# Expert weights of a MoE block: loads that take fourteen places in rotation, with two places more

## The reference

```
g_sel     = argmax(h @ w_router_group + b)             # one of 4 groups per token
top_idx   = top_k(e_logits of that group, 2)           # two of its 8 experts per token
for e in 32 experts:
    ys[e] = (silu(x_e @ w_gate[e]) * (x_e @ w_up[e])) @ w_down[e]   # 1024 -> 256 -> 1024
out       = x + sum over the two experts of weight * ys
result    = rmsnorm(out)
```

## Time and profile before

| | us |
|---|---|
| median of 3 runs (lowest, highest) | 1531.02 (1529.89, 1532.00) |
| profiled execution | 1532.88 |
| its span, first to last instruction | 1531.1 |
| PE busy in the span | 1417.8 (93%) |
| DVE busy | 898.7 (59%) |
| ACT busy | 620.6 (41%) |
| DMA, mean over the span | 248 GB/s |

### The profile page before, as it was taken

How to read it: one execution, slowest core, us unless ns; L and a number is a source line. 1 busy time by engine, 2 the same in 40 slices (tenths; PEclk the granted TensorE clock), 3 DMA queues, 4 the chain that set the end, 5 groups by cost and what they waited for, 6 DMA issues and landing times.

```text
span 1531.1 us, 26859 instructions
## 1 busy us (share of the span) xinstructions
PE 1417.8 (93%) x11511; PEld 1272.0 (83%) x11511; DVE 898.7 (59%) x1043; ACT 620.6 (41%) x739; POOL 19.2 (1%) x24
## 2 busy tenths in 40 slices
PE   4999999999999999999999999999999999985665
PEld 2899998988999989999999899999997989652323
DVE  2777776547877777777775555556567644320002
ACT  2444345545444354344443443444444643320002
POOL 0000000400000000000000000000000000000000
PEclk9899999999999999999999999999999999998879
DMA  8898884515988849788654355554534349799996
GB/s 308 276 324 301 303 306 165 198 56 200 324 306 301 296 165 329 274 287 307 202 167 164 111 195 190 192 176 136 175 108 147 129 157 405 308 422 421 421 421 267
DMA packets 203911, 380.33 MB, mean 248 GB/s; under 512 B 12725, under 2 KB 158010, under 8 KB 192058
## 3 DMA queue, kind: packets, MB, share of 16 engines
q1 hardware_dynamic: 203834, 379.22, 69.1%
HBM read 378.14 MB, written 1.05 MB: 248 GB/s over the span
## 4 chain that ended last, share of the span: by engine, by line
PE 80%; DMA 9%; DVE 5%; ACT 3%; issue 2%; SPq 1%; ACTq 0%; DVEq 0%
PE ps L678 18%; PE ps L680 17%; PE ps L679 17%; PE ps L706 10%; DMA plain_whi<-in_w_exp_down_dram 7%; PE ps L707 5%; PE ps L1427 2%; ACT whi L1540 2%; DVE wlo L1964 2%; DMA ada_raw<-in_w_ada_dram 1%; PE ps L1400 1%; PE ps L1383 1%; SPq L561 1%; PE ps L846 1%; PE ps L793 1%
## 5 line engine op out<-in xcount | busy, mean ns | idle before, releaser
L1964 DVE TENSOR_TENSOR wlo<-raw,whi 128x2048 fp32r<-128x2048 f32 (+1 forms) x188 | 425.5, 2263 | 241.2 <-ACT whi L1540 241.1
L1540 ACT ACTIVATE whi<-raw 128x2048 fp32r<-128x2048 f32 (+1 forms) x188 | 354.7, 1887 | 175.4 <-PE ps L680 146.7
L678 PE MATMUL ps<-h_both,whi 128*128 128x256 f32 x1320 | 380.4, 288 | 1.2 <-DVE wlo L1964 0.9
L680 PE MATMUL ps<-h_both,wlo 128*128 128x256 f32 x1320 | 374.5, 284 | 0.0
L679 PE MATMUL ps<-h_both,whi 128*128 128x256 f32 x1320 | 374.4, 284 | 0.0
L678 PEld LDWEIGHTS ps<-h_both,whi 128*128 128x128 f32 x1320 | 252.0, 191 | 9.4 <-issue 4.5
L706 PE MATMUL ps<-h_both,whi 128*128 128x512 f32 x704 | 254.8, 404 | 2.1 <-DVE h_both L1974 2.1
L679 PEld LDWEIGHTS ps<-h_both,whi 128*128 128x128 f32 x1320 | 252.2, 191 | 0.7 <-issue 0.5
L680 PEld LDWEIGHTS ps<-h_both,wlo 128*128 128x128 f32 x1320 | 252.1, 191 | 0.0
L678 PE MATMUL ps<-hidhi,whi 128*128 128x256 f32 x704 | 201.2, 286 | 2.1 <-DVE wlo L2101 2.1
L680 PE MATMUL ps<-hidhi,wlo 128*128 128x256 f32 x704 | 199.3, 283 | 0.0
(11 more groups left out here) (325 smaller groups left out, 1851.4 us busy)
## 6 DMA issues: line engine op xcount, KB each, us to landing
ada_raw<-in_w_ada_dram SPq DMA_DIRECT2D x72, 1024.0 KB, 5.4
raw<-in_ffn_wg_dram SPq DMA_DIRECT2D x44, 1024.0 KB, 6.0
raw<-in_ffn_wu_dram SPq DMA_DIRECT2D x44, 1024.0 KB, 5.4
raw<-in_ffn_wd_dram SPq DMA_DIRECT2D x44, 1024.0 KB, 6.3
raw<-in_w_in_dram SPq DMA_DIRECT2D x18, 1024.0 KB, 5.3
raw<-in_w_exp_down_dram SPq DMA_DIRECT2D x14, 1024.0 KB, 19.0
plain_whi<-in_w_exp_gate_dram SPq DMA_DIRECT2D x14, 1024.0 KB, 19.0
plain_wlo<-in_w_exp_gate_dram SPq DMA_DIRECT2D x14, 1024.0 KB, 16.9
```

Of the source, the lines that this page charges most:

```text
L678: pe.matmul(o, wh, xh, start=start, stop=False, skip_group_check=shared)
L680: return pe.matmul(o, wl, xh, start=False, stop=stop, skip_group_check=shared)
L1540: act.activation(whi[s][:, 0:width], raw[s][:, 0:width], ACT.Copy).then_inc(high[s], 1)
L1964: dve.tensor_tensor(wlo[s][:, 0:width], raw[s][:, 0:width], whi[s][:, 0:width].bitcast(F32), ALU.subtract).then_inc(split[s], 1)
```

## The change

The program now reserves 2 KB of each partition of SBUF for DMA descriptors (`dynamic_dma_scratch_size=2048` in the call at L2634, where no size was given before), and two places of 8 KB each, `spare[0]` and `spare[1]`, are allocated. Three things follow in the order of the loads.

First, the loads of GATE(0) for j = 0 and 1 go into the two spare places, and SP issues them between units of `blk2`, behind u = 20 and u = 22. Before, they stood behind u = 30.

Second, in round 1 the loads of UP for j = 1 and 2 go into `ar(0)` and `ar(4096)`, which held those of GATE(0) before. They wait for no product, only for the landing of the load of round 0 that has the same semaphore.

Third, from UP(1), j = 3 on, the loads take fourteen places (`ring`) in turn. Load m of this rotation waits for the product that last read its place (`ring_user`), and for the landing of the load before on its own semaphore. In the old code a load waited for the product of its own kind in the round before.

```diff
+        spare = [sb(f"spare{i}", [P, UW]) for i in range(2)]
...
-        first_w = [[ar(0, UW), ar(4096, UW), ar(6144, UW), plain_over("exps")],
+        first_w = [[spare[0][:, :], spare[1][:, :], ar(6144, UW), plain_over("exps")],
...
-                    [h_area[1], ar(6144, UW), raw[2][:, :], ada_raw[:, 0, :]],
-                    [ada_raw[:, 1, :], raw[0][:, :], raw[1][:, :], split_area["whi2"]]]
-        later_w = [[split_area[name] for name in ("wlo2", "whi0", "wlo0", "whi1")],
-                   [split_area["wlo1"], ar(6144, UW), raw[2][:, :], ada_raw[:, 0, :]],
-                   [ada_raw[:, 1, :], raw[0][:, :], raw[1][:, :], split_area["whi2"]]]
+                    [h_area[1], ar(0, UW), ar(4096, UW)]]
+        ring = [spare[0][:, :], spare[1][:, :], ar(6144, UW), raw[2][:, :], ada_raw[:, 0, :], ada_raw[:, 1, :]] + \
+               [split_area[name] for name in ("whi0", "wlo0", "whi1", "wlo1")] + \
+               [raw[0][:, :], raw[1][:, :], split_area["whi2"], split_area["wlo2"]]
+        RING_AT = 12 + 4 * UP + 3
...
+        def ring_user(m):
+
+            if m < len(ring):
+                return (((GATE, 1),) * 3 + ((UP, 1),) * 3 + ((GATE, 2),) * 4 + ((DOWN, 1),) * 4)[m]
+            q, rest = divmod(m - len(ring) + RING_AT, 12)
+            return rest // 4, q + 1
...
+            for u in range(31):
+                load_unit("blk2", u)
+                if u in (20, 22):
+                    expert_load(0, GATE, u // 2 - 10)
+
             sp.wait_ge(sem("o_split"), 8)
-            expert_load(0, GATE, 0)
-            expert_load(0, GATE, 1)
+            expert_load(0, GATE, 2)
             load_unit("blk2", 31)
-            expert_load(0, GATE, 2)
             expert_load(0, GATE, 3)
...
-            expert_load(1, UP, 0)
-            sp.wait_ge(expert_used[GATE], 1)
-            expert_load(1, UP, 1)
-            sp.wait_ge(expert_used[UP], 1)
-            expert_load(1, UP, 2)
-            expert_load(1, UP, 3)
-            expert_load(1, DOWN, 0)
-            sp.wait_ge(expert_used[DOWN], 1)
-            for j in range(1, 4):
-                expert_load(1, DOWN, j)
-            for q in range(2, NQ):
-                for kind in (GATE, UP, DOWN):
-                    sp.wait_ge(expert_used[kind], q)
-                    for row in ((0, 1) if kind == DOWN and q == NQ - 1 else (None,)):
-                        for j in range(4):
-                            expert_load(q, kind, j, row=row)
+            for j in range(3):
+                sp.wait_ge(expert_landed[UP][j], 16)
+                expert_load(1, UP, j)
+            for m in range(ring_index(NQ, GATE, 0)):
+                q, rest = divmod(m + RING_AT, 12)
+                kind, j = divmod(rest, 4)
+                user, uses = ring_user(m)
+                sp.wait_ge(expert_used[user], uses)
+                sp.wait_ge(expert_landed[kind][j], 16 * q)
+                expert_load(q, kind, j, row=0 if (q, kind) == (NQ - 1, DOWN) else None)
+            for j in range(4):
+                expert_load(NQ - 1, DOWN, j, row=1)
```

More of the change, by code:

```diff
@@ L287, in build, with ring_index @@
         second_w = [[split_area[name] for name in ("whi0", "wlo0", "whi1", "wlo1")],
-                    [h_area[1], ar(6144, UW), raw[2][:, :], ada_raw[:, 0, :]],
-                    [ada_raw[:, 1, :], raw[0][:, :], raw[1][:, :], split_area["whi2"]]]
-        later_w = [[split_area[name] for name in ("wlo2", "whi0", "wlo0", "whi1")],
-                   [split_area["wlo1"], ar(6144, UW), raw[2][:, :], ada_raw[:, 0, :]],
-                   [ada_raw[:, 1, :], raw[0][:, :], raw[1][:, :], split_area["whi2"]]]
-        def expert_w(q, kind, j):
-            return (first_w, second_w, later_w)[min(q, 2)][kind][j]
+                    [h_area[1], ar(0, UW), ar(4096, UW)]]
[3 more added lines that the diff above has]
+        RING_AT = 12 + 4 * UP + 3
+        def ring_index(q, kind, j):
+            return 12 * q + 4 * kind + j - RING_AT
+        def expert_w(q, kind, j):
+            if q == NQ:
+                q = NQ - 1
+            m = ring_index(q, kind, j)
+            if m >= 0:
+                return ring[m % len(ring)]
+            return (first_w, second_w)[q][kind][j]
+        def ring_user(m):
[3 more added lines that the diff above has]
+            return rest // 4, q + 1
         y_hi = sb_over("y_hi", "hf", 0, [P, D])
@@ L547, in _ @@
             dense("ffn3", 1, 1, None)
-            for u in range(31):
-                load_unit("blk2", u)
             def expert_load(q, kind, j, e=None, row=None):
@@ L2632 @@
     from concourse.bass_utils import run_bass_kernel_spmd as _run
-    nc = _bacc.Bacc("TRN2", target_bir_lowering=False, num_devices=1)
+    nc = _bacc.Bacc("TRN2", target_bir_lowering=False, num_devices=1, dynamic_dma_scratch_size=2048)
     arrays, aps = {}, {}
```

## The result

| | before | after |
|---|---|---|
| median of 5 runs each (lowest, highest), us | 1531.02 (1529.89, 1533.31) | 1523.75 (1520.24, 1525.04) |
| profiled execution, us | 1532.88 | 1525.04 |
| its span, us | 1531.1 | 1523.2 |

The ratio is 0.9948, with a 95% interval of 0.9935 to 0.9961. The median is 7.3 us lower; 1524.4 had been forecast, and 1523.75 was measured. Busy times are the same within 0.6 us (PE 1417.2, DVE 898.7, ACT 620.1 us), so nothing is computed faster.

What follows compares the result with a forecast made beforehand. The end of a byte stream at 421 GB/s was taken to bound the kernel. Two loads (5.0 us) plus closed holes (1.6 us) make 6.6 us less, 1524.4 us against the median of 1531.02; 8-in-10 range 1521.5 to 1527.5.

Steps and rivals of the forecast that it cites:

- What bounds the kernel: At the kernel's end, a stream of bytes at 421 GB/s bounds; the 13.6 us after the last landing stay untouched.
- The unit: In the load stream, one load of 1024 KB takes the full stream 2.49 us at 421 GB/s.
- Part 1: Two GATE(0) loads issued early in blk2: cost nothing and give nothing; the stream would stand idle longer before 1314.
- Part 2: Before GATE(0): two more UP(1) loads issued, 5.0 us less stream behind 1314; dead stretch begins at 1311 or 1312.
- Part 3: At the restart after GATE(0): more loads released, two holes close, 1.05 us and 0.58 us, 1.6 us together.
- Part 4: In the rotation up to GATE(2)'s end near 1361: the queue just lasts, 0.3 us to spare, nothing lost.
- the first rival: Around 1363: PE brings GATE(2) late and the stream goes dry; 1526 to 1527.5 us; chance 0.09.
- Part 5: The 2 KB descriptor area in SBUF: loads run on a hardware queue, so its effect is taken as 0.
- The sum: Whole kernel: 5.0 + 1.6 = 6.6 us less, 1524.4 against the median; bounds 5.0 and about 9.
- Slow issuing: In the rotation: a deeper queue makes SP's issues set the pace; 1536.7 us at 2.65 per load; chance 0.04.
- The loads of UP(1) got out: Before 1314: the rival said an earlier wait holds these two loads, only holes gained; 1529.4 us; chance 0.04.
- signs of being wrong: Wrong if the GATE(0) product itself moved, the rate fell below 421, or the stream went dry in a later round.

Runs made afterwards that it cites:

- e5: The changed kernel, but the load of UP(1), j = 2 waits for GATE(0); 1525.21 us in one run.
- e6: The changed kernel, but the loads of UP(1), j = 1 and 2 wait for GATE(0); 1528.15 us in one run.
- e1: The changed kernel, but the first two loads of GATE(0) are issued at their old place behind unit 30 of blk2; 1523.30 us, ratio to before 0.9956.
- e2: The kernel before, with only the spare places, the 2 KB area and the early issue of two GATE(0) loads; 1531.67 us, ratio 1.0005.
- e7: The changed kernel, but the second and third of the three loads that GATE(0) releases wait for UP(0); 1526.14 us in one run.
- e11: The kernel of e7 once more, unchanged; 1526.96 us in one run.
- e9: The changed kernel once more, with a profile; 1523.42 us in one run.
- e3: The changed kernel, but from round 2 on each load also waits for its own kind's product in the round before; 1526.46 us, ratio to before 0.9972.
- e8: The kernel before once more, with a profile; 1529.49 us in one run.
- e4: The changed kernel, but five eighths of the load of UP(1), j = 3 go ahead of the wait for GATE(0); 1524.86 us, ratio to before 0.9959.

## Why the prediction was right

*What bounds the kernel.* Right: the last landing fell by what the stream gained, and what follows it took 13.5 us as before.

*The unit, 2.49 us.* Right: 2.58 and 5.07 us at the end of the bytes for one and two loads (e5, e6). On the 358 GB/s that the prediction sets beside it, the same page of the Trainium skill ("DMA: Bandwidth & Descriptors", section on measured bandwidth) is fuller than the prediction tells: it gives 358 GB/s for a core when both cores of the pair stream. For a single core whose neighbour is idle it gives 425 GB/s, measured for a transfer of 16 MB, and the 421 of this program, which uses one core, agree with that.

*Part 1, the early issue at nothing.* Right in the time, from both sides (e1, e2). The idle time came in the front and not, as I had it, as a longer dead stretch (e2). This was the step at which the plain reading of the change, two loads earlier, two loads gained, would have come out right by chance and for a wrong reason.

*Part 2, 5.0 us.* Right: 5.07 (e6). The dead stretch began at about 1311, as forecast.

*Part 3, 1.6 us.* Nearly right: with both loads of UP(1) held back, the end of the bytes is still 203.83 - 202.52 = 1.3 us ahead of before. The hole of the restart alone is 0.9 to 1.1 (e7, e11), where 1.05 was forecast. The second hole, put at 0.58, has no run of its own.

*Part 4, nothing lost at 1361.* Right, and in the profile of after with more room than I had worked out. GATE(2) ended at 1354.45 + 3.63 = 1358.1 and not at 1361, 1.2 us of it from the start of GATE(0), and the rest because PE's clock was less low on the way. The same window of before and then of after (PE busy, granted clock, DMA share, GB/s):

```profile
1328.00:1340.00 12.00, 12.00 (x109) 0.72 1.01 425
```
```profile
1328.00:1340.00 12.00, 11.52 (x119) 0.86 1.01 420
```

That second part was luck of the execution and doesn't belong to the change. In e9, the changed kernel again, the clock was as low as in before, and GATE(2) ended 1354.51 + 3.63 - 1307.79 = 50.35 us after the start of GATE(0), where before has 50.37 and after 48.73 (the second window has all engines, columns as in the earlier trace rows):

```profile
1325.22:1337.22 12.00, 12.00 (x110) 0.72 1.01 421
```
```profile
1354.00:1364.00 10.00, 9.74 (x139) 5.45 (x137) 1.54 (x3) 1.65 (x3) 0.00 (x0) 1.00 1.01 416
```

So e9 is the narrow case of the forecast. There is no hole where the first rival has one, and the ruler is the same (200.33).

What I had not said is what the rotation is worth: 2.6 us of bytes against the old rule (e3). The old rule has 36 loads issued when GATE(2) ends, and with the gains of parts 2 and 3 these are through 6.6 us sooner than before, which is too soon. The forecast needed the 38 loads issued by then without naming them as a gain.

*Part 5, the area.* The rate stayed at 421 GB/s with the smaller area (e2, after).

*The sum, 6.6 us.* 6.57 on the ruler, and 203.83 - 197.45 = 6.38 at the end of the bytes: 5.07 for the two loads and 1.31 for the order behind them. The other 0.2 is a shorter lag, so that the ruler meets 6.6 so closely is partly chance. The medians differ by 7.3; the rest is within what the start of GATE(0) varies by.

*The rivals.* Slow issuing did come as a sight, 2.09 us for one load at 1427.55, and the stream ran at 421 GB/s through it: a full queue pushing back, and not a pace. The loads of UP(1) got out. PE's waits for landings behind 1370 shrank from 47.6 us to 39.9, and the stream never ran dry. One of my signs of being wrong did come, GATE(0) starting 1.2 us earlier; e8 and e9 show that such a shift comes without the change, too.

## What to carry to other kernels

When a stream of loads is the bound and it stands still somewhere, count the loads issued before the stop: each one more was worth its full transfer time here (2.5 us, by two steps), and it needs a free place, not an earlier issue of the same loads. Loads moved into idle time ahead of a stop that covers them gave nothing. Then look at the first product behind the restart whose places the queue needs: the one hole there cost 2.6 us, as much as a load (e3). Part of a load, cut off and issued ahead of the stop, gave less than its share (e4).

## What was not expected of the hardware

- The last landing came 2.9 to 3.2 us behind the end of the bytes at full rate in nine of thirteen profiled executions. With a hole of some 2.6 us in the stream 150 us earlier it was 1.8 and 1.9, in e4 it was 3.4, and once (e7) it was 3.9 without a reason that I found. The packets in flight show the engines of the core ending their parts up to 4 us apart. A change in the bytes of less than 1 us can vanish in it.
- The start of GATE(0), after 1300 us of the same work, varied by 5.4 us between executions (1305.2 to 1310.6), at least in part by how long PE's clock stayed halved after a wait: at the same place of the program (838 to 844 us) it was 0.50 and 0.56 once, 0.64 and 1.00 the other time.
